# Stream-split norms of a two-network kernel: a conditioning tile held back, two row sums moved by a block, one weight split moved between two rows

## What is computed

```python
for i in range(DEPTH_2):                       # 4 layers
    mod_l = silu_c @ mod_w[i] + mod_b[i]       # shifts, scales, gates; likewise mod_c
    a_l = modulate(rmsnorm(x, norm1_g[i]), mod_l[:, 0], mod_l[:, 1])   # likewise a_c from ctx
    y_l, y_c = mixer(a_l, a_c)                 # attention (0, 3), conformer (1), short conv (2)
    x = x + mod_l[:, 2] * y_l
    m_l = modulate(rmsnorm(x, norm2_g[i]), mod_l[:, 3], mod_l[:, 4])
    x = x + mod_l[:, 5] * sq_relu_mlp(m_l, mlp_w1[i], mlp_w2[i])
    ...                                        # the same for ctx in layers 0 to 2
```

## Time and profile before

| | |
|---|---|
| median of three executions | 3056.82 us |
| the profiled execution | 3052.42 us, span 3050.6 us |
| PE (matmuls) busy | 95% of the span |
| DVE, ACT, POOL busy | 66%, 39%, 12% |
| mean granted clock of PE | 0.981 |
| chain that ended last | PE 83%, DVE 9%, ACT 4% |

### The profile page before, as it was taken

How to read it: one execution, slowest core, us unless ns; L and a number is a source line. 1 busy time by engine, 2 the same in 40 slices (tenths; PEclk the granted TensorE clock), 3 DMA queues, 4 the chain that set the end, 5 groups by cost and what they waited for, 6 DMA issues and landing times.

```text
span 3050.6 us, 42744 instructions
## 1 busy us (share of the span) xinstructions
PE 2908.1 (95%) x17730; PEld 2516.9 (83%) x17730; DVE 2002.3 (66%) x3252; ACT 1197.9 (39%) x1953; POOL 351.9 (12%) x545
## 2 busy tenths in 40 slices
PE   7998999979999989999999899999999999898898
PEld 7998998879977758888864788888888888876898
DVE  6675786658745557777653676777777667554665
ACT  5444444644444434233322642223234222343543
POOL 0000001000112310000122100001010000234000
PEclk9999999989999999999999999999999999999999
DMA  6443576437755523555464255553545545465353
GB/s 216 150 139 125 196 238 195 141 114 251 235 127 86 95 49 118 166 159 159 131 175 131 82 161 159 159 166 118 163 127 166 159 156 169 116 95 93 126 191 127
DMA packets 362276, 451.88 MB, mean 148 GB/s; under 512 B 12657, under 2 KB 332433, under 8 KB 362081
## 3 DMA queue, kind: packets, MB, share of 16 engines
q1 hardware_dynamic: 326976, 329.89, 33.3%
q0 software_dynamic: 34944, 118.65, 16.6%
q10 hardware_dynamic: 160, 0.59, 0.1%
HBM read 438.67 MB, written 1.05 MB: 144 GB/s over the span
## 4 chain that ended last, share of the span: by engine, by line
PE 83%; DVE 9%; ACT 4%; issue 1%; DMA 1%; POOL 1%; DVEq 0%; ACTq 0%; POOLq 0%
PE ps L1134 24%; PE ps L1135 24%; PE ps L1136 24%; PE ps L1312 2%; PE ps L1155 1%; DVE lo L1641 1%; PE ps L1156 1%; PE ps L1157 1%; DVE lo L1644 1%; PE ps L1299 1%; DVE NB L1675 1%; PE ps L1287 1%; ACT hi L1344 1%; PE ps L1267 1%; PE ps L1167 1%
## 5 line engine op out<-in xcount | busy, mean ns | idle before, releaser
L1134 PE MATMUL ps<-XN,hi 128*128 128x256 f32 (+1 forms) x3120 | 1038.4, 333 | 52.2 <-DVE XN L1888 11.3
L1135 PE MATMUL ps<-XN,hi 128*128 128x256 f32 (+1 forms) x3120 | 1020.8, 327 | 0.0
L1136 PE MATMUL ps<-XN,lo 128*128 128x256 f32 (+1 forms) x3120 | 1020.7, 327 | 0.0
L1134 PEld LDWEIGHTS ps<-XN,hi 128*128 128x128 f32 x3120 | 599.9, 192 | 129.8 <-issue 13.7
L1136 PEld LDWEIGHTS ps<-XN,lo 128*128 128x128 f32 x3120 | 600.0, 192 | 49.0
L1135 PEld LDWEIGHTS ps<-XN,hi 128*128 128x128 f32 x3120 | 600.7, 193 | 47.3
L1641 DVE TENSOR_TENSOR lo<-raw,hi 128x1024 fp32r<-128x1024 f32 (+1 forms) x313 | 383.6, 1226 | 260.2 <-ACT hi L1344 258.8
L1720 DVE CUSTOM_DVE_ANT_0 MX<-MW,C 128x1024 bf16<-128x1024 f32 x384 | 481.2, 1253 | 110.3 <-DMA MW<-in_mod_w 103.5
L1344 ACT ACTIVATE hi<-raw 128x1024 fp32r<-128x1024 f32 (+1 forms) x313 | 326.2, 1042 | 429.6 <-PE ps L1136 428.4
L1134 PE MATMUL ps<-H,hi 128*128 128x512 f32 (+1 forms) x1072 | 382.9, 357 | 0.0
L1135 PE MATMUL ps<-H,hi 128*128 128x512 f32 (+1 forms) x1072 | 381.2, 356 | 0.0
(11 more groups left out here) (239 smaller groups left out, 3406.9 us busy)
## 6 DMA issues: line engine op xcount, KB each, us to landing
raw<-in_mlp_w SPq DMA_DIRECT2D x128, 1024.0 KB, 5.3
MW<-in_mod_w POOLq DMA_DIRECT2D x192, 512.0 KB, 3.8
raw<-in_ffn_w_in SPq DMA_DIRECT2D x44, 1024.0 KB, 5.4
raw<-in_attn_w_in SPq DMA_DIRECT2D x36, 1024.0 KB, 4.8
raw<-in_na_wqkv SPq DMA_DIRECT2D x24, 1024.0 KB, 5.5
raw<-in_ffn_w_out SPq DMA_DIRECT2D x16, 1024.0 KB, 5.4
raw<-in_mlstm_w_in SPq DMA_DIRECT2D x12, 1024.0 KB, 5.2
raw<-in_cv_w SPq DMA_DIRECT2D x12, 1024.0 KB, 6.9
```

Source lines behind the costliest of these rows:

```text
L1134: e.matmul(out, whi, xhi, start=first, stop=False)
L1135: e.matmul(out, whi, xlo, start=False, stop=False)
L1136: i = e.matmul(out, wlo, xhi, start=False, stop=last)
```

## The change

Three edits to the order of steps; no instruction is added or removed. First, `beside` may be told to hold: after the last output tile ahead of a closing unit no conditioning tile is emitted, and the credit stays for the next call. Second, in `close` the first pending sum of stream 0 is no longer issued after the blocks of t = 1; both sums of stream 0 are issued after three blocks of stream 1 (k = 0 to 2), where the second stood after four. Third, in `norm_streams`, for layer 3 alone, the pending split is emitted after the last step of row 0 and not by the next `take` behind row 1.

```diff
-    def beside(self):
+    def beside(self, hold=False):
         self.credit = min(self.credit + self.pace / 2, 2.0)
-        if self.credit >= 1:
+        if self.credit >= 1 and not hold:
             self.credit -= 1
             self.condition()
...
             if not (outer or quiet):
-                self.beside()
+                self.beside(hold and t == tiles[-1])
...
                     self.do("product", j, t, k, KT, (b, u), ("part", x, i), k == 0, k == KT - 1, True, i == 1)
-                    if i == 1 and t == 0 and k == 3:
+                    if i == 1 and t == 0 and k == 2:
                         self.flush()
-                if (i, t) != (1, 0):
+                if i == t:
                     self.flush()
-                else:
+                elif i:
                     self.do("rstd_part", s, 0, *sums[0], self.rs_user)
...
                 self.do("rest_part", s, k, i, shift)
                 if (i, k) == (0, 1):
                     end()
+                if (i, k) == (0, KT - 1) and split_between:
+                    self.splits()
...
-    s = p.norm(512, ("gs", layer, 0), (layer, 0))
+    s = p.norm(512, ("gs", layer, 0), (layer, 0), not ctx_out)
...
-            p.linear("cv_w2_2", 0, 0, KT, c * 256, 256, ("cn", 0, 0, 512), evac, outer=c == 0)
+            p.linear("cv_w2_2", 0, 0, KT, c * 256, 256, ("cn", 0, 0, 512), evac, outer=c == 0, hold=c == 2)
```

More of the change, by code:

```diff
@@ L359, in reads, with linear @@
             self.xn_used = [("used", j), ("used", j)]
-    def linear(self, w, layer, k0, kt, c0, cols, x, evac, adv=1, outer=False, until=None, quiet=False, streams=None):
+    def linear(self, w, layer, k0, kt, c0, cols, x, evac, adv=1, outer=False, until=None, quiet=False, hold=False, streams=None):
         j = self.take(w, layer, k0, kt, c0, cols)
@@ L471, in rstd, with norm @@
         return s
-    def norm(self, n, gain, shift=None):
+    def norm(self, n, gain, shift=None, split_between=False):
         if self.tail:
-            return self.norm_streams(gain, shift)
+            return self.norm_streams(gain, shift, split_between)
         self.flush()
@@ L490, in norm, with norm_streams @@
         return s
-    def norm_streams(self, gain, shift):
+    def norm_streams(self, gain, shift, split_between):
         self.conditions_for(shift[0], shift[1] + 1)
@@ L538, in grow @@
             self.linear(w, layer, 0, KT, c * 256, 256, x, evac, adv=adv if first else 1, outer=bool(first),
-                        until=first, quiet=c == 3)
+                        until=first, quiet=c == 3, hold=c == 2 and n == 512)
             if first:
@@ L949, in down @@
                 p.linear("mlp_w2_2", layer, q * D, KT, c * 256, 256, ("h2", layer, q, n), evac,
-                         quiet=q == 3 and c == 3)
+                         quiet=q == 3 and c == 3, hold=(q, c, n) == (3, 2, 512))
     up(0)
```

## The result

| | before | after |
|---|---|---|
| median | 3056.9 us (4 executions, 3054.8 to 3057.1) | 3035.05 us (4 executions, 3031.3 to 3038.2) |
| ratio | | 0.9930, 95% interval 0.9912 to 0.9947 |
| profiled execution | 3052.42 us | 3036.18 us, span 3034.4 us |

The changed kernel is 21.8 us faster (16 to 27 by the interval), where 20.0 were forecast, and the time of 3035.05 lies 1.8 us under the predicted 3036.8.

A forecast was written before the change was run, and what follows sets the result against it. PE, busy 95% of the span, was taken to bound the kernel. Sums 6.1, held tile 2.8, clock 4.6 and split 6.5 made 20.0 us off 3056.8, so 3036.8 us, range 3032 to 3045.

The forecast's parts named there:

- Edit 1: First sums of stream 0, six closings: three more blocks ahead save 1.08 us each, less 0.4 after the conformer: 6.1 us.
- Edit 2: Fourth and sixth closing: without the conditioning tile, POOL's sum SA comes 1.39 us earlier, 2.8 us in all.
- The clock: Second, fourth and sixth closing: shorter waits keep PE's granted clock at 1.00, about 1.5 us each, 4.6 us.
- Rival (b): Clock dips move elsewhere instead of going; the three closings' 4.6 us come back: 3041.4 us, chance 0.14.
- Edit 3: Layer 3's split between the rows: keys unit starts 4.75 us earlier, runs 2.6 faster; 6.5 us taken, bounds 3.0 to 7.4.
- what the tables take: Layer 3's bias tables come at least 2.9 us earlier, PE wants them 7.35 earlier; PE keeps 3.0 to 7.35.
- some 3 us: Layer 3's table 0: the part of its 9.77 us DMA wait it might get back, letting PE keep all 7.35.
- the narrowest place: Layer 3's table 3: ready at 2696.20, used at 2698.35, with 2.15 us to spare.
- (a): Layer 3's bias tables take back the split's gain; PE keeps 3 of 6.5 us: 3040.3 us, chance 0.15.
- (c): Layer 3: the split's place does nothing, ACT's `hi` being late for another reason; gain 0, 3043.3 us, chance 0.05.
- (d): Slower: layer 3's tables 2 to 13 each take 12.9 us beside weight loads: 3068 us, chance 0.02.

The follow-up runs named there:

- hold_only: Kernel before with only the conditioning tile held after the last output tile ahead of a closing; sums and split as before: 3047.74 us, ratio 0.9975.
- split_only: Kernel before with only layer 3's split moved between the rows; sums as before and no held tile: 3045.90 us, ratio 0.9964.

## Why the prediction was right, point by point

**Edit 1, 6.1 us: right.** 1.03 to 1.07 us in each of the closings 1, 2, 5 and 6, by legs free of low clock. After the conformer the second sum starts 0.73 behind the first (1727.57 and 1728.30) where it is 0.54 in the sixth closing, so 0.2 us were lost there, not 0.4: the spacing of the two sums had been put at 0.35.

**Edit 2, 2.8 us: right,** 1.40 and 1.37. In DVE's timeline of the changed kernel the split stands right behind ACT's half in the sixth closing, as in the earlier trace rows, and the tile is seen in layer 3's values unit:

```profile
2611.55 1.41 DVE L1643 TENSOR_TENSOR lo<-raw,hi 128x1024 fp32r<-128x1024 f32 x1 [1.72 <-ACT hi L1346]
...
2646.71 1.22 DVE L1722 CUSTOM_DVE_ANT_0 MX<-MW,C 128x1024 bf16<-128x1024 f32 x1
```

**The clock, 4.6 us: right in this pair of traces, wrong as a price.** All three stretches behind the closings are gone, and closing 2's leg shows it (2.62 us shorter, 1.07 of them the sums). But the 1.5 us of the second closing were luck of the first trace: behind a wait of 1.87 us the clock fell in 1 of 8. Priced by the table above, before had 3 x 0.7 + 2 x 0.125 = 2.35 such stretches in an execution and the changed kernel 2/7, so at 8.50 - 6.94 = 1.56 us each the change saves an estimated 3.2 us on average, not 4.6. The step that failed is the reading of one trace's three stretches as standing costs. Rival (b) was partly right in that: a dip isn't tied to its place. (The windows that the price was read from hold the 16 blocks of stream 1 and six matmuls of sums, 54 in all, and not 24 blocks; they hold the same work, so the price stands.)

**Edit 3, 6.5 us: under-sized.** It gave 4.76 + 2.56 = 7.3, all of the 7.35 that the forecast held possible. The 4.75 up to the keys unit were hit, down to the wait of 1.45. ACT and DVE stand as forecast (`hi` at 2637.4, `lo` at 2638.5, row 1's end at 2646.5), all 9.0 us earlier by what had been gained up to the sixth closing. ACT's `hi`:

```profile
2628.39 1.04 ACT L1346 ACTIVATE hi<-raw 128x1024 fp32r<-128x1024 f32 x1
```

DVE, `lo` and the end of row 1:

```profile
2629.53 1.23 DVE L1643 TENSOR_TENSOR lo<-raw,hi 128x1024 fp32r<-128x1024 f32 x1 [1.20 <-ACT hi L1346]
...
2636.17 1.27 DVE L1683 SCALAR_TENSOR_TENSOR XN<-NB,mod,XN 128x256 fp32r<-128x256 f32 x3
```

The term that was sized wrongly is what the tables take. Tables 0 and 1 waited 8.52 and 4.21 us for their DMAs, against 9.77 and 6.41 before: 3.45 us less, the "some 3 us" that the forecast held possible and didn't count in full. The single edits don't give it to the split alone: table 1 waits 4.11 us in hold_only and 5.31 in split_only (6.4 in both executions of before), and table 0 waits 9.8 to 10.0 in both, 8.5 and 9.3 in the two executions of the changed kernel. POOL's timeline, the moved load and tables 2 and 3:

```profile
2659.31 0.57 POOL L2065 DMA_DIRECT2D MW<-in_mod_w  x1
...
2668.16 2.98 POOL L2110 TENSOR_TENSOR NB<-NB,cst 128x256 f32<-128x256 f32 x2 [5.63 <-DMA NB<-in_na_rpb]
...
2678.00 1.43 POOL L2110 TENSOR_TENSOR NB<-NB,cst 128x256 f32<-128x256 f32 x2 [4.49 <-DMA NB<-in_na_rpb]
```

Scores 3 in DVE's timeline answer:

```profile
2682.04 0.68 DVE L1925 CUSTOM_DVE_ANT_0 PB<-ps,NB 128x512 f32<-128x512 f32 x1
```

Table 3 is ready at 2679.43, 2.6 us ahead of scores 3 (2.15 before). The moved load of 0.57 us costs nothing there. But naming table 3 as the narrowest place was wrong. The delayed tables failed at table 1 first, which has 2.95 us to spare in the changed kernel, and a DMA wait that came out 3.5 longer. And the last table had nothing to spare before the change either: the last scores wait for POOL in every trace, for 0.3 to 2.9 us. Before and changed:

```profile
2821.45 0.69 DVE L1923 CUSTOM_DVE_ANT_0 PB<-ps,NB 128x512 f32<-128x512 f32 x1 [2.93 <-POOL NB L2108]
...
2805.02 0.69 DVE L1925 CUSTOM_DVE_ANT_0 PB<-ps,NB 128x512 f32<-128x512 f32 x1 [2.66 <-POOL NB L2110]
```

This table's load is released by scores 13, so it moves along with them. The wait comes in the same two sizes in both kernels (2.93 and 0.98 us before, 2.66 and 0.98 changed), so it took nothing from the gain.

**The rivals.** (a) didn't happen, but with 4 us more on POOL it would have. (c) is out: the place of the split is worth 7 us alone. (d) is out: tables 2 to 13 come 10.5 us apart, no slower than before (11.0, from table 1's end to table 13's; the forecast's 10.4 starts at table 2's issue). **The sum** by measured parts is 1.07 x 6 - 0.2 = 6.2 for the sums, 2.8, 3.2 on average for the clock, and 7.3: 19.5 us. That this is so near the forecast's 20.0 is in part luck: the clock was priced 1.4 us too high, edit 3 0.8 too low. The two comparisons gave 21.8 and 24.9 (intervals 16 to 27 and 20 to 27), the legs 20.6 and 17.2. The two to five us by which the medians exceed the sum stay open; the part that no edit touches moves by as much from one execution to the next.

## What to carry to other kernels

Price an edit by the same leg of several executions, and take for its base a leg in which the clock didn't fall: differences of single traces credited one and the same low stretch to several edits. Before moving a step, look for the first reader of what it delays; the same move is worth 7 us where 16 blocks or more lie between and costs 4 to 5 us each time where none do. When work is deferred rather than removed, follow the counter that brings it back: one held tile cost nothing, two cost more than all that the other edits of that version won.

## What the runs showed of the hardware

Behind the first sums, the granted clock after a short wait of PE went both ways, and the more often to 0.50 the longer the wait: never behind 59 waits of up to 1.44 us, 3 times behind 15 of 1.5 to 1.9, 7 times behind 10 of 2.5 to 2.6. So an estimate from these counts is that cutting a wait of 2.5 us below 1.4 saves 0.7 x 1.56 = 1.1 us on top of the wait itself. And a delay on POOL's queue isn't always passed through unchanged: 4.0 us came out as 7.2 us on the second table behind it, since the table's DMAs were then waited for 7.75 us in place of 4.21, while 8.1 us came out as 8.5 (a wait of 4.81). Why the one wait grew and the other hardly did isn't shown.
